# Last stage of a two-block transformer kernel on one Trainium2 core: embedding products, gate products and output turning reordered

## The reference, cut to what matters

```
x = x + rms_norm(hid @ w_down, g_ffn_post)                      # sixth norm: x3 -> x4
ple_gate = sigmoid(rms_norm(x, g_ple_gate) @ w_ple_gate)        # seventh norm, "gate products"
ple = rms_norm(p @ w_ple_proj, g_ple_post)                      # "embedding products", eighth norm
x = x + ple_gate * ple
```

## Time and profile before

| what | value |
|---|---|
| time, median of 3 | 3582.59 us |
| the profiled execution: time | 3582.84 us |
| the profiled execution: span from first to last instruction | 3581.1 us |
| PE busy | 3191.9 us (89%) |
| DVE busy | 2170.1 us (61%) |
| ACT busy | 1322.4 us (37%) |
| POOL busy | 1028.4 us (29%) |

### The profile page before, as it was taken

The page is one execution under the profiler, slowest core; times in us unless marked ns, Lnnn a source line. Parts: engine busy times, 40 slices in busy tenths (PEclk is TensorE's granted clock), DMA queues, the critical chain, the costliest instruction groups (busy, mean ns, idle before and its releaser), DMA issues. The chain is left out here.

```text
span 3581.1 us, 45184 instructions
## 1 busy us (share of the span) xinstructions
PE 3191.9 (89%) x15078; PEld 2527.7 (71%) x15078; DVE 2170.1 (61%) x2771; ACT 1322.4 (37%) x1726; POOL 1028.4 (29%) x529
## 2 busy tenths in 40 slices
PE   5889988888886399999959999699799999999868
PEld 4658866555674388888848788588588888888647
DVE  6588875786524599999865655633555154154362
ACT  3345423666302388888720364101311000001141
POOL 2223322000231211111124333344244444344332
PEclk9999999999998699999979999899899999999989
DMA  6312221230231599999961122132311111111213
GB/s 223 82 42 89 71 59 47 95 110 10 88 129 56 218 385 381 376 379 386 345 237 47 59 88 66 31 115 79 112 56 50 47 47 50 50 47 47 102 57 117
DMA packets 348590, 454.47 MB, mean 127 GB/s; under 512 B 33662, under 2 KB 230204, under 8 KB 348484
## 3 DMA queue, kind: packets, MB, share of 16 engines
q1 hardware_dynamic: 334420, 422.68, 34.2%
q10 hardware_dynamic: 4192, 13.63, 1.3%
q0 software_dynamic: 9872, 16.81, 1.3%
HBM read 401.58 MB, written 62.98 MB: 130 GB/s over the span
## 5 line engine op out<-in xcount | busy, mean ns | idle before, releaser
L405 PE MATMUL acc<-Ah,whi 128*128 128x512 f32 x2336 | 934.0, 400 | 74.5 <-DVE Al L599 18.5
L377 POOL TENSOR_TENSOR whi<-wraw,one 128x1024 fp32r<-128x1024 f32 (+3 forms) x214 | 394.3, 1842 | 1868.1 <-PE acc L407 1533.8
L406 PE MATMUL acc<-Al,whi 128*128 128x512 f32 x2336 | 918.5, 393 | 0.0
L407 PE MATMUL acc<-Ah,wlo 128*128 128x512 f32 x2336 | 918.3, 393 | 0.0
L405 PEld LDWEIGHTS acc<-Ah,whi 128*128 128x128 f32 x2336 | 443.7, 190 | 193.9 <-issue 69.9
L379 POOL TENSOR_TENSOR wlo<-wraw,whi 128x1024 fp32r<-128x1024 f32 (+3 forms) x214 | 532.9, 2490 | 16.8
L406 PEld LDWEIGHTS acc<-Al,whi 128*128 128x128 f32 x2336 | 444.1, 190 | 97.0 <-issue 5.1
L407 PEld LDWEIGHTS acc<-Ah,wlo 128*128 128x128 f32 x2336 | 443.4, 190 | 95.2
L1785 DVE TENSOR_TENSOR mlo<-mraw,mhi 128x1024 fp32r<-128x1024 f32 x256 | 306.3, 1224 | 36.5 <-ACT mhi L1735 25.1
L1735 ACT ACTIVATE mhi<-mraw 128x1024 fp32r<-128x1024 f32 x256 | 266.7, 1062 | 73.1 <-PE acc L1680 45.9
L405 PE MATMUL acc<-Bh,whi 128*128 128x512 f32 x640 | 251.2, 393 | 9.1 <-POOL wlo L379 9.1
(11 more groups left out here) (446 smaller groups left out, 4785.0 us busy)
## 6 DMA issues: line engine op xcount, KB each, us to landing
mraw<-in_exp_w SPq DMA_DIRECT2D x512, 256.0 KB, 6.5
mraw<-in_exp_w SPq DMA_DIRECT2D x128, 512.0 KB, 12.0
wraw<-in_w_in SPq DMA_DIRECT2D x72, 512.0 KB, 3.7
wraw<-in_w_up SPq DMA_DIRECT2D x48, 512.0 KB, 3.7
TT<-in_ada_w SPq DMA_DIRECT2D x32, 512.0 KB, 3.7
TT<-gates SPq DMA_DIRECT2D x32, 512.0 KB, 4.4
wraw<-in_w_down SPq DMA_DIRECT2D x24, 512.0 KB, 3.5
adaraw<-in_ada_w SPq DMA_DIRECT2D x16, 512.0 KB, 8.5
```

Of the source, the lines that this page charges most:

```text
L377: ch(pool.tensor_tensor(whi[:, r, 0:k, 0:m], wraw[:, r, 0:k, 0:m], one[:, 0:1].unsqueeze(2).broadcast_to([P, k, m]), ALU.mult))
L405: pe.matmul(o, whi[:, r, j, 0:m], ih[:, k0 + j, cols], start=(j == 0), stop=False)
L406: pe.matmul(o, whi[:, r, j, 0:m], il[:, k0 + j, cols], start=False, stop=False)
L407: last = pe.matmul(o, wlo[:, r, j, 0:m], ih[:, k0 + j, cols], start=False, stop=(j == k - 1))
```

## The change

- `p` is loaded when the last feed-forward chunk's first half is done, and is turned and split between the first and the second of the last eight feed-forward products, through two other PSUM banks (`p_banks`). x3 is loaded tile by tile during these products, into `Al`.
- The embedding products are queued right behind the last feed-forward product, and copied by ACT to `PL`; the sixth norm's mean stands behind the second of them.
- The DVE loop after norm six makes, for each tile, scale, add x3, and the low part of gain times x4, without the seventh root. ACT makes the high part, the square for norm seven, and from tile 4 on two squares of the embedding result. The first gate product runs behind this loop tile by tile, with a mean matmul after each.
- The seventh root is multiplied on the results of the gate products by DVE (`gate_raw`) before the sigmoid. DVE sums the squares of norm eight around the Newton step of norm seven; the mean of norm eight stands on PE between the second and the third gate product.
- x4 stays in `C`; its store and load are gone.
- The output is finished tile by tile, turned by feature block between the gate products, and stored in pieces of 512 bytes.

The diff, cut to its core:

```diff
+    p_banks = (XX, Y)
...
+                for m in range(KD):
+                    load(sp, n0 + 16 + m, m % 2, WDN[:, c * KD:(c + 1) * KD, m * P:(m + 1) * P])
+                    if m == 1:
+                        sp.wait_ge(w_used, n0 + 16)
+                        sp.dma_start(PR[:], A["p_2"][0, 0].rearrange("(b p) n -> p b n", p=P)).then_inc(S("p_in"), 16)
+                    for b in ((), (), (), (0, 1), (2, 3), (4, 5), (6,), (7,))[m]:
+                        sp.dma_start(X3[:, b, :], x3T[b * P:(b + 1) * P, :]).then_inc(S("x3T_in"), 16)
+                load_run(sp, N0["plep"], 8, lambda m: WPP[:, :, ds(m * P, P)], k=2)
+                load_run(sp, N0["pleg"], 8, lambda m: WPG[:, :, ds(m * P, P)])
...
             product(pe, n0 + 16, 0, Bh, Bl, free=take(0), ready=(S("hid_lo"), 8 * c))
+            if c == CH - 1:
+                pe.wait_ge(S("p_in"), 16)
+                for k in range(2):
+                    for b in range(NB):
+                        last = pe.transpose(p_banks[k][:, b * P:(b + 1) * P], PR[:, b, k * P:(k + 1) * P], ident[:])
+                    last.then_inc(S("p_turned"), 1)
...
     @block.tensor
+        def square_mean(j):
+            pe.wait_ge(S("n7_sq"), j + 1)
+            add_mean(pe, TT[:, j % 2, :], j == 0, j == KD - 1, "n7_sum")
+        def turn(m):
+            pe.wait_ge(S("result"), m + 1)
+            if m >= 2:
+                pe.wait_ge(S("out_row"), m - 1)
+            for b in range(NB):
+                last = pe.transpose(p_banks[m % 2][:, b * P:(b + 1) * P], C[:, m, b * P:(b + 1) * P], ident[:])
+            last.then_inc(S("out_turned"), 1)
         pe.wait_ge(S("p_lo"), 2)
-        product_run(pe, N0["plep"], 8, pTh, pTl, 2)
+        for m in range(2):
+            product(pe, N0["plep"] + m, m, pTh, pTl, 2, free=take(m))
+        pe.wait_ge(S("n6_sum"), KD)
+        add_mean(pe, TT[:, 2, :], True, True, "n6_mean")
+        product_run(pe, N0["plep"] + 2, 6, pTh, pTl, 2)
+        pe.wait_ge(S("n6_root_used"), 1)
+        product(pe, N0["pleg"], 0, Ah, Al, free=take(0), ready=(S("n7_lo"), 0), after=square_mean)
+        product(pe, N0["pleg"] + 1, 1, Ah, Al, free=take(1))
+        pe.wait_ge(S("n8_sum"), 1)
+        pe.wait_ge(S("n7_root_used"), 1)
+        add_mean(pe, S8, True, True, "n8_mean")
+        for m in range(2, KD):
+            product(pe, N0["pleg"] + m, m % 2, Ah, Al, free=take(m % 2))
+            for t in ((), (), (), (0,), (1, 2), (3,), (4, 5), (6, 7))[m]:
+                turn(t)
...
     @block.scalar
+        plep_out(0)
+        plep_out(1)
+        root(act, "n6", R6, ("n6_mean", 1))
+        plep_out(2)
+        plep_out(3)
+        for m in range(KD):
+            if m < 4:
+                plep_out(m + 4)
+            act.wait_ge(S("n6_added"), m + 1)
+            split_rows("n7", m, act=act, gain=gain7)
+            if m >= 2:
+                act.wait_ge(S("n7_sum"), m - 1)
+            act.activation(TT[:, m % 2, :], C[:, m, :], ACT.Square).then_inc(S("n7_sq"), 1)
+            if m >= 4:
+                for p in (2 * m - 8, 2 * m - 7):
+                    ch(act.activation(BG[:, p, :], PL[:, p, :], ACT.Square))
+                    act.sem_inc(S("n8_sq"), 1)
+        root(act, "n7", R7, ("n7_sum", KD))
+        root(act, "n8", R8, ("n8_mean", 1))
+        for m in range(KD):
+            act.wait_ge(S("gate_raw4"), m + 1)
+            ch(act.activation(TT[:, m % 2, :], TT[:, m % 2, :], ACT.Sigmoid))
+            act.sem_inc(S("ple_gate"), 1)
+            for t in ((), (), (), (0,), (1, 2), (3,), (4, 5), (6, 7))[m]:
+                turned_out(t)
...
     @block.vector
+        for m in range(KD + 1):
+            if m < KD:
+                ch(dve.scalar_tensor_tensor(C[:, m, :], C[:, m, :], vec("g_ffn_post_2", m), R6, ALU.mult, ALU.mult))
+                ch(dve.tensor_tensor(C[:, m, :], C[:, m, :], X3[:, m, :], ALU.add))
+                dve.sem_inc(S("n6_added"), 1)
+            if m:
+                split_rows("n7", m - 1, dve=dve, gain=gain7)
+        for p in range(1, 5):
+            square_sum(p)
+        newton_step(dve, ch, "n7", R7, TT[:, 2, :])
+        dve.sem_inc(S("n7_root_used"), 1)
+        gate_raw(0)
+        for p in range(5, KD):
+            square_sum(p)
+        dve.sem_inc(S("n8_sum"), 1)
+        gate_raw(1)
+        newton_step(dve, ch, "n8", R8, BG[:, 2, :])
         for m in range(KD):
+            ch(dve.scalar_tensor_tensor(PL[:, m, :], PL[:, m, :], vec("g_ple_post_2", m), R8, ALU.mult, ALU.mult))
             dve.wait_ge(S("ple_gate"), m + 1)
+            ch(dve.tensor_tensor(PL[:, m, :], PL[:, m, :], TT[:, m % 2, :], ALU.mult))
+            ch(dve.tensor_tensor(C[:, m, :], C[:, m, :], PL[:, m, :], ALU.add))
+            dve.sem_inc(S("result"), 1)
+            if m + 2 < KD:
+                gate_raw(m + 2)
...
     @block.sync
+        for m in range(KD):
+            sp.wait_ge(S("out_row"), m + 1)
+            sp.dma_start(OUT[:, :, m * P:(m + 1) * P], rows_out(m).rearrange("p (b n) -> p b n", b=NB))\
+              .then_inc(S(f"out_st{m % 4}"), 16)
```

More of the change, by code:

```diff
@@ L2392, in _ @@
                     dve.sem_inc(S("down"), 1)
+                    if m == 0:
+                        for k in range(2):
+                            dve.wait_ge(S("p_hi"), k + 1)
+                            ch(dve.tensor_tensor(pTl[:, k, :], p_banks[k][:], pTh[:, k, :].bitcast(F32), ALU.subtract))
+                            dve.sem_inc(S("p_lo"), 1)
                     if m:
@@ L2414, in _ @@
                 ch.leave(4)
[L2416 to L2464, removed]
+    gain7 = lambda m: vec("g_ple_gate_2", m)
+    R6, R7 = TT[:, 2, :], TT[:, 3, :]
+    S8, R8 = BG[:, 0, :], BG[:, 1, :]
+    rows_out = lambda m: BG[:, 4 + m % 4, :]
+    OUT = out[0].rearrange("(b p) n -> p b n", p=P)
     @block.gpsimd
@@ L2472, in _ @@
     def _(pe):
-        pe.wait_ge(S("p_lo"), 2)
-        product_run(pe, N0["plep"], 8, pTh, pTl, 2)
[L2476 to L2488, removed]
+        def square_mean(j):
+            pe.wait_ge(S("n7_sq"), j + 1)
+            add_mean(pe, TT[:, j % 2, :], j == 0, j == KD - 1, "n7_sum")
@@ L2490, in _ @@
     @block.scalar
     def _(act):
-        for m in range(KD):
-            act.wait_ge(w_used, N0["pleg"] + m + 1)
-            ch = chain(act, "act")
-            ch(act.activation(BG[:, m, :], acc[m % 2][:], ACT.Sigmoid))
-            act.sem_inc(acc_free[m % 2], 1)
-            act.sem_inc(S("ple_gate"), 1)
[L2498 to L2502, removed]
+        ch = chain(act, "act")
@@ new lines, in _, with plep_out @@
+        for k in range(2):
+            act.wait_ge(S("p_turned"), k + 1)
+            act.activation(pTh[:, k, :], p_banks[k][:], ACT.Copy).then_inc(S("p_hi"), 1)
+        act.preload_act_table_set(LN_EXP)
+        for m in range(KD):
+            act.wait_ge(S("down"), m + 1)
+            if m >= 2:
+                act.wait_ge(S("n6_sum"), m - 1)
+            act.activation(TT[:, m % 2, :], C[:, m, :], ACT.Square).then_inc(S("n6_sq"), 1)
+        def plep_out(m):
+            act.wait_ge(w_used, N0["plep"] + m + 1)
+            ch(act.activation(PL[:, m, :], acc[m % 2][:], ACT.Copy))
+            act.sem_inc(acc_free[m % 2], 1)
@@ new lines, in square_sum, with gate_raw @@
+        def square_sum(p):
+            dve.wait_ge(S("n8_sq"), p + 1)
+            ch(dve.tensor_tensor(S8, S8, BG[:, p, :], ALU.add))
+        def gate_raw(m):
+            dve.wait_ge(w_used, N0["pleg"] + m + 1)
+            ch(dve.tensor_tensor(TT[:, m % 2, :], acc[m % 2][:], R7, ALU.mult))
+            dve.sem_inc(acc_free[m % 2], 1)
+            dve.sem_inc(S("gate_raw4"), 1)
+        for p in range(1, 5):
+            square_sum(p)
+        newton_step(dve, ch, "n7", R7, TT[:, 2, :])
+        dve.sem_inc(S("n7_root_used"), 1)
@@ L2511, in _ @@
             dve.wait_ge(S("ple_gate"), m + 1)
-            ch(dve.tensor_tensor(C[:, m, :], C[:, m, :], BG[:, m, :], ALU.mult))
-            ch(dve.tensor_tensor(C[:, m, :], C[:, m, :], RG[:, m, :], ALU.add))
-        dve.sem_inc(S("result"), 1)
-    @block.tensor
-    def _(pe):
-        pe.wait_ge(S("result"), 1)
-        for b in range(NB):
-            pe.wait_ge(acc_free[b % 2], take(b % 2))
-            for m in range(KD):
-                last = pe.transpose(acc[b % 2][:, m * P:(m + 1) * P], C[:, m, b * P:(b + 1) * P], ident[:])
-            last.then_inc(S("out_turned"), 1)
+            ch(dve.tensor_tensor(PL[:, m, :], PL[:, m, :], TT[:, m % 2, :], ALU.mult))
@@ L2532, in program @@
+        for r in range(4):
+            sp.wait_ge(S(f"out_st{r}"), 32)
     stage.close()
```

34 lines of the change are left out of this document (21 added, 13 removed).

## The result

The changed kernel takes 3551.1 us (median of 4 runs, 3546.1 to 3554.8), the kernel before 3580.8 in the same comparison: a ratio of 0.9915, with a 95% interval of 0.9903 to 0.9927. The forecast was 3554 in a range of 3538 to 3567.

The account below looks back on a forecast made before the run. The prediction took the last 206.6 us as bound by relays between engines around 87 us of gate products; its seven steps sum to 177.9, 28.7 us less, so 3582.8 becomes 3554, range 3538 to 3567.

Parts of the forecast that it names:

- 1 turning p: Between two of the last feed-forward products: 16 transposes on TensorE's path add 2.3 us, with p loaded in about 6.
- 2 to the first scaled tile: From the last feed-forward product to the first scaled tile: 13.8 us as before, later mean start and faster mean even.
- 3 DVE's loop: First scaled to last added tile: 37.2 us, being 28.6 plus 7.6 for two weight splits and 1.0 for small ones.
- 4 to norm eight's sum: Last added tile to norm eight's sum: 26.1 us with two splits at 3.8 each; TensorE waits 6.9 us.
- 5 its mean: Norm eight's mean matmul: 3.4 us, since TensorE comes from 6.9 us of idle time.
- 6 gate products 2 to 7, turns 0 to 5: 79.3 us: products 65.3, turns 0 to 3 at 1.14 each, 6.4 between products 6 and 7, restarts 1.0 and 2.0.
- 7 tail: Behind gate product 7 to the end of the span: 15.8 us instead of 20.0, nothing added for 512-byte store pieces.
- Rival (b): p lands late for its transposes before the last feed-forward products, costing 4.8 us: 3559 us; chance 0.05.
- Rival (a): GpSimd's splits in steps 3 and 4 fall beside other work, costing DVE nothing: 3536 us; chance 0.28 whole or in part.
- (c): Turn groups before gate products 4, 5 and 6 each make TensorE restart its clock, 2.2 us each: 3561 us; chance 0.06.
- (e): TensorE stays at 1.2 GHz from gate product 4 on because of the transposes, 38.4 us longer: 3592 us; chance 0.02.
- Rival (d): The first gate product doesn't run behind DVE's loop, its eight tiles follow it: +22 us, 3576, no change; chance 0.03.

Follow-up runs that it names:

- skip01: Changed kernel with GpSimd's splits of gate weights 0 and 1 left out (old weights used): 3543.6 us, ratio 0.9897 to the kernel before.
- means_first: Changed kernel with gate product 0 whole behind norm seven's mean matmuls instead of interleaved with them: 3553.3 us, ratio 0.9918 to the kernel before.
- turn5: Changed kernel with output turn 5 moved behind gate product 7, beside turns 6 and 7: 3542.9 us, ratio 0.9900 to the kernel before.

## Why the prediction was right, step by step

| step | forecast | measured |
|---|---|---|
| 1 turning p | 2.3 | 1.8 |
| 2 to the first scaled tile | 13.8 | 13.4 |
| 3 DVE's loop | 37.2 | 37.4 |
| 4 to norm eight's sum | 26.1 | 27.0 |
| 5 its mean | 3.4 | 3.7 |
| 6 gate products 2 to 7, turns 0 to 5 | 79.3 | 77.6 |
| 7 tail | 15.8 | 16.1 |
| sum | 177.9 | 177.0 |

The stage took 206.6 us before, so it gained 29.6 of the forecast 28.7; the rest of the difference of the two profiled spans is the 3.0 us ahead of the stage, which the medians, 29.7 apart, don't show. That the sum is off by only 0.9 us is in part luck: step 6 is 1.7 below its forecast and step 4 is 0.9 above.

1. The additions behind feed-forward products 1 and 2 stand 12.64 us apart (3295.41 and 3308.05) instead of 10.88. p was there in time: TensorE shows no idle time before the transposes, and the load landed after 5.4 us where about 6 was estimated. Rival (b) is out.
2. The mean ran at the full clock behind the embedding products (1.88 us instead of 3.28), and that more than paid for the 1.0 us by which it started later.
3. The cost of the two splits, 7.6 us by the earlier trace rows, is the term on which the sum hung, and skip01 measured 7.1. Rival (a) is out. The first split began 9.2 us into the loop, where it waited last for its weights (0.7 us) and not for a product. The Trainium skill (SBUF — State Buffer, Who interferes with whom) says that the second to issue is blocked in full, and the trace agrees: each of the four DVE operations beside these halves ends 1.08 or 1.09 us after its half, so it waited the half out. Six halves of the small splits met the loop, not about four, and its operations beside them took 1.39 to 1.76 us. That is 1.7 us in all where the prediction had 1.0, and with the 0.5 too much above it nearly cancels. These six also end 1.07 to 1.09 us after their halves. They lost only 0.1 to 0.5 because they came late in a half, so the prediction was wrong to read the rule as a whole small half lost each time.
4. The last high part was late by more than I had: 5.7 us to the last low part instead of 4.3. ScalarE's 4.4 us per tile were foreseen; a wait for TensorE was not. TensorE stood idle for 2.19 us behind a low part that the splits had held up, its next matmuls stood 0.43 instead of 0.23 us apart, the mean of tile 2 took 2.38 instead of 1.88 us, and ScalarE's square of tile 4 waited 1.37 us for it. In means_first, where no product stands between these means, the last low part comes at 4.2. This wait of ScalarE, in front of a high part, is of the kind that the prediction named as a sign of being wrong; it was small. The wait of TensorE for the sum was forecast at 6.9 and is 7.0.
5. As forecast, at the lower clock (0.53 in that stretch).
6. Mis-sized in small parts that cancel: a turn in the running stream 0.9 instead of 1.14; no restart at product 2, since the mean took all of it; 1.3 instead of 2.0 at product 7; but turn 5 itself at the lower clock, so 7.4 instead of 6.4 between products 6 and 7.
7. As forecast. The store in pieces of 512 bytes landed after 3.2 us (median) instead of 2.8, and the last copy's end to the end of the span was 3.7.

Rivals (c) and (e): in the 47.2 us of products 3 to 6 with turns 0 to 3 between them the granted clock was 1.00. The sentence of the Trainium skill (TensorE: Matmul & The Clock Gate, Part 4: PE-mode transpose) that transposes don't engage the full clock has no trace here of a cost; the clock fell only after idle time. Rival (d) didn't occur. Its price put the product and its means together behind the loop, for 22 us, and no run tests that; means_first moves the product alone, and that costs nothing in this kernel. What I had not said, though step 4 had the numbers for it (TensorE done at 19.2, the sum at 26.1), is that a part of the change was without effect because of this wait.

How the 29.6 us divide among the other parts of the change (p turned ahead, the embedding products behind the last feed-forward product, the seventh root on the results) no run shows: only the interleaving and the end of the kernel were undone alone.

## What to carry to other kernels

When work is moved beside a norm, list what the other engines release in that stretch: here GpSimd's weight splits, freed by the very products that were moved, cost DVE 3.6 us each. Read an engine's order for waits that stand in front of work that doesn't need them (the mean before gate product 2, gate_raw(m + 2) before tile m + 1): the two, put right with no work removed, were worth 18.6 us, nearly two thirds of what the whole rebuild gained. And judge a part of a change by undoing it alone before and after the next wait is gone: the interleaved product was worth 0 with the wait and 8 us without.

## What the runs showed of the hardware

TensorE's restart after an idle time of the same length (4.5 us before turn 5) cost from 1.3 to 2.0 us in five kernels with the same instructions there, so a difference below 1 us in such a stretch can't be put down to an edit. Eight transposes took 1.04 us in a running stream and mostly 1.97 after 4.55 us of idle time, but 1.60 in turn5 (turn 6).

A DVE operation with both inputs in SBUF that started beside a half of a split ended 1.07 to 1.09 us after that half, wherever in the half it had started: so in all 19 single rows of this kind in the stage of the changed kernel, ten of them in the loop. GpSimd's halves stretched too: the large ones took up to 3.26 us (1.9 and 2.4 where DVE had nothing beside them), the small ones up to 1.60 (0.61 and 0.74). What one split costs DVE depends on what DVE does at the time: with operations whose inputs all lie in SBUF it lost 3.4 and 3.7 us in the loop and 3.6 in each group of square sums, but beside the gate products only 2.3 (1.55 and 3.30 us for operations of 1.29 and 1.23), where the first half met gate_raw, which reads one input from PSUM and kept its own length. DVE of the changed kernel, in time, behind gate product 3; the split's halves ran from 3476.69 to 3478.59 and from 3478.67 to 3481.93:

```profile
3476.65 1.23 DVE L2558 TENSOR_TENSOR TT<-acc,TT 128x1024 f32<-128x1024 f32 x1 [3.27 <-PE acc L407]
3478.12 1.55 DVE L2573 SCALAR_TENSOR_TENSOR RG<-RG,VEC,BG 128x1024 f32<-128x1024 f32 x1 [0.24 <-DVE TT L2558]
3479.70 3.30 DVE L2575 TENSOR_TENSOR RG<-RG,TT 128x1024 f32<-128x1024 f32 x1
```
